# Tokens 0 to 127 of an expert gate built by indexed adds in DRAM instead of one-hot matmuls

## The chip, the cores and the metric

The kernel runs on one core of a Trainium2 chip. The metric is the device time of one launch in microseconds. Before the change it is 2061.44 us, the median of three runs (2060.55 to 2062.73).

## The reference

A decoder trunk of 256 tokens by 1024 features and 2 layers. Each layer has a mixer, a cross-attention and an expert block with 128 x 128 single-neuron experts, and 8 heads that choose 16 experts per token. The change is in the expert block:

```python
q = (xb @ w_pq).reshape(PEER_BLOCK, P_HEADS, 2, P_HALF)
sc = jnp.einsum('thpc,hpkc->thpk', q, sub_keys)
sv, si = lax.top_k(sc, TOPK)
cand = (sv[..., 0, :, None] + sv[..., 1, None, :]).reshape(..., TOPK * TOPK)
cid = (si[..., 0, :, None] * N_KEYS + si[..., 1, None, :]).reshape(..., TOPK * TOPK)
fv, fi = lax.top_k(cand, TOPK)
eid = jnp.take_along_axis(cid, fi, axis=-1)
g = jax.nn.softmax(fv, axis=-1)
a = gelu(einsum('thkd,td->thk', u_experts[eid], xb))
y = einsum('thk,thkd->td', g * a, v_experts[eid])
```

## The kernel before

The kernel does not gather experts. It computes the block densely: h = gelu(U x) for all 16384 experts, times a gate that is zero where a token did not choose an expert and the sum of its softmax weights where it did, times V. Weights come in slabs of 512 KB (128 partitions x 1024 float32), 340 a layer: 84 for the projections, 128 of U, 128 of V. SP loads them into a ring of four (`raw`). ACT rounds a slab to `w_hi` (fp32r), DVE makes the rest `w_lo` (`lo_part`, L848), and TensorE uses both: per U slab 8 chunks of one 512-column and one 256-column matmul (`wide_chunk`, L1345 and L1346), per V slab 12 matmuls of 512 columns (`expert_out`, L1733). The next slab into a ring place is asked for once its `lo_part` is through.

For each U slab ACT copies half of the sums to `h_out` (L721), DVE adds the other half (L1113), ACT applies gelu (L731), and SP stores 128 KB to `h_park` in DRAM. During V, SP loads these rows back into `h_in` (the first three into `early_in`), GpSimd multiplies each by its gate row (`gated`, L524), ACT and DVE split the product (L781, L1264), and TensorE uses it as the stationary operand.

The gate is `gate[column, row, token]` in SBUF, 128 KB per partition. While U streams, DVE finds the top 16 of the scores and of the candidate sums (`top16`), then decodes the row and the column of each choice with 16 comparisons (`pick`, L1198) and a tree of additions (L1206) for all 16 (token block, head) pairs at once, and makes the softmax weights (L1211 to L1213, semaphore `decoded`). Between these steps a helper `spend` puts the `lo_part`s into DVE's order: one whenever the estimated time of the other work has reached 1.56 us. At U slab `RET_AT` = 70 TensorE transposes rows, columns and weights (L1697, six 128x128). From slab `HOT_AT` = 72 on, DVE makes one-hot matrices for groups of 4 tokens (L1228, L1236, L1242), TensorE multiplies them (`gates_of`, L1708, 8 matmuls a group), and ACT copies the result to `gate` (L761). There are 64 groups a layer, in pairs, placed by `GROUP_AT` at fixed chunks of slabs 72 to 123: a pair every 13 chunks. The last four U slabs follow (L1339). TensorE, DVE, ACT, SP and GpSimd each have one order of instructions, written out in the program, and meet by semaphores.

GpSimd does little in U: after the sums of squares (L494), the load of `skT` (L507) and a scaling (L476) it waits for the last one-hot group, loads `par` (L516), and starts on `gated`.

Of the kernel before, what the change touches and what calls it, by code (L numbers as in the profile page):

```python
# [45 lines left out]
PH = 8  # L46
# [53 lines left out]
GROUPS = T // 4  # L100
HOT_AT = 72
RET_AT = 70
EXP_AT = 60
# [5 lines left out]
GROUP_AT = tuple(FIRST_PAIR + (n - n % 2) * HOT_SLABS * KB // GROUPS for n in range(GROUPS))  # L109
EARLY = RING - 1  # L110
H_SLOTS = 2
# [38 lines left out]
def trunk(nc, x, mem, slabs, params, sub_keys, out):  # L150
    ctx = ExitStack()
    with ctx:
# [32 lines left out]
        h_out = at("h_out", x_at + 6144, [P, H_SLOTS, T])  # L185
# [17 lines left out]
        pick_at = at("pick_at", top[0], [P, 2, T // 2, 2], FP16)  # L203
        g_parts = at("g_parts", top[0] + 2 * T * 2, [P, T // 2, PARTS, 2], FP16)
        top[0] += (2 + PARTS) * T * 2
        top[0] = (top[0] + LINE - 1) // LINE * LINE
        gated_at = top[0]
        gate = sb("gate", [P, NKEYS, T])
# [78 lines left out]

        h_park = nc.dram_tensor("h_park", (NKEYS, P, T), FP32, kind="Internal").ap()
# [7 lines left out]
        def sem(name):  # L296
            return ctx.enter_context(nc.semaphore(name))
# [39 lines left out]
        settled = sem("settled")  # L337
        act_step, dve_step, out_ready = sem("act_step"), sem("dve_step"), sem("out_ready")
# [12 lines left out]
        def _(sp):  # L351
# [26 lines left out]
            for layer in range(DEPTH):  # L378
# [10 lines left out]
                for j in range(RING):  # L389
                    next_slab(layer, U_AT, 0, j)  # L390
                    if j >= H_SLOTS:
                        store_h(layer, 0, j - H_SLOTS, j - H_SLOTS)
                with sp.Fori(1, U_SLABS // RING - 1) as g:
                    for j in range(RING):
                        next_slab(layer, U_AT, g, j)
                        store_h(layer, g, (j - H_SLOTS) % RING, j - H_SLOTS)
                last = U_SLABS // RING - 1
                for j in range(RING):
                    next_slab(layer, U_AT, last, j)
                    store_h(layer, last, (j - H_SLOTS) % RING, j - H_SLOTS)  # L400
# [9 lines left out]
                for j in range(H_SLOTS):  # L410
                    next_slab(layer, V_AT, 0, j)
                    store_h(layer, U_SLABS // RING, j, j - H_SLOTS)
# [7 lines left out]
                next_slab(layer, V_AT, 0, H_SLOTS)  # L420
# [37 lines left out]
        def _(pool):  # L458
# [11 lines left out]

            def scale(dst, count, evacs, xns):
# [25 lines left out]
            for layer in range(DEPTH):  # L497
# [7 lines left out]
                sum_chunks(layer, SUM_OUT, 0)  # L505
                pool.wait_ge(slab_done, layer * SLABS + XO_AT)
# [5 lines left out]
                settle(pool)  # L512

# [6 lines left out]
                def gated(g, j, h, n):  # L520
# [3 lines left out]
                    nc.gpsimd.tensor_tensor(h[:, n:n + 1, :], h[:, n:n + 1, :], gate[:, ds(g * RING + j, 1), :],  # L524
# [17 lines left out]
        def _(act):  # L542
# [73 lines left out]
            for layer in range(DEPTH):  # L616
# [89 lines left out]
                def gelu_out(at0, g, j):  # L706

                    act.wait_ge(slab_done, layer * SLABS + U_AT + at0 + g * RING + j + 1)
                    act.wait_ge(h_stored[j % H_SLOTS], (layer * (U_SLABS // H_SLOTS) + at0 // 2 + g * 2 + j // 2) * 16 + 16)
# [7 lines left out]
                def half_of(at0, g, j):  # L717

                    act.wait_ge(slab_done, layer * SLABS + U_AT + at0 + g * RING + j + 1)
                    act.wait_ge(h_stored[j % H_SLOTS], (layer * (U_SLABS // H_SLOTS) + at0 // 2 + g * 2 + j // 2) * 16 + 16)  # L720
# [30 lines left out]
                experts(RING, EXP_AT - RING)  # L751
                act.wait_ge(fin_ready, layer + 1)
                nc.scalar.activation(g_exp[:], g_exp[:], ACT.Exp).then_inc(gexp_ready, 1)
                experts(EXP_AT, HOT_AT - RING - EXP_AT)
# [4 lines left out]
                def gate_out(n):  # L759
                    act.wait_ge(gate_mm, layer * GROUPS + n + 2)  # L760
                    nc.scalar.activation(gate[:, :, 4 * n:4 * n + 4],  # L761
# [80 lines left out]
        def _(dve):  # L842
# [119 lines left out]
            for layer in range(DEPTH):  # L962
# [179 lines left out]
                for n in range(0, TB * SETS, 2):  # L1142
                    if n % SETS == 0:
                        dve.wait_ge(sc_evac, layer * TB + n // SETS + 1)
                        settle(dve)
                    src = (scores0, scores1)[n // SETS]
                    step.join()
                    top16(*[(src[:, m % SETS, :], struck[:, m - n, 0:NKEYS], top_v[:, m, :], top_u[:, m, :])
                            for m in (n, n + 1)], us=0.29)
                step.join()  # L1150
                step.mark(nc.vector.tensor_copy(top_i[:], top_u[:]))

                step.join()
                for b in range(TB):
                    tops = top_v[:, b * SETS:(b + 1) * SETS, :].rearrange("p (h s) a -> p h s a", s=2)
                    step.join()
                    first = 0
                    for a0, na, nb in CAND:
                        shape = [P, PH, na, nb]
                        step.mark(nc.vector.tensor_tensor(  # L1160
                            cand[:, :, first:first + na * nb].rearrange("p h (a b) -> p h a b", a=na),
# [3 lines left out]
                    spend(1.3)  # L1165
                    for n in range(b * PH, (b + 1) * PH, 2):
# [3 lines left out]
                step.join()  # L1170

                nc.vector.tensor_tensor(g_exp[:], fin_v[:], fin_v[:, :, 0:1].to_broadcast([P, TB * PH, TOPK]),
                                        ALU.subtract).then_inc(fin_ready, 1)
                flat_i = fin_i[:].rearrange("p c k -> p (c k)")
                step.mark(nc.vector.tensor_scalar(bit_u[:], flat_i, 8, None, ALU.bitwise_and))
                step.mark(nc.vector.tensor_scalar(low_u[:], flat_i, 7, None, ALU.bitwise_and))
                step.mark(nc.vector.tensor_scalar(by16_u[:], flat_i, 4, None, ALU.logical_shift_right))
# [638 lines left out]
```

## Time and profile before

| | us |
|---|---|
| median of three runs | 2061.44 |
| the profiled execution | 2061.37 |
| its span, first to last instruction | 2059.6 |
| TensorE busy | 2042.0 |
| DVE busy | 1643.4 |
| ACT busy | 1190.0 |
| GpSimd busy | 337.0 |

The profiled execution is within 0.1 us of the median, and 1.8 us of it lie outside the span. "Busy" counts an instruction from start to end, and matmuls overlap, so the durations of matmuls can't be added; the distance between starts says what one costs. All positions below are microseconds from the start of the span, in the first layer.

### The profile page before, as it was taken

What the parts mean: (1) busy time and instruction counts of PE and PEld (TensorE: products, weight loads), DVE (VectorE), ACT (ScalarE), POOL (GpSimd) and SP (SyncE); (2) the same over time, 40 slices, a digit from 0 to 9 for tenths busy, and PEclk for the clock granted to TensorE, in tenths of its full rate; (3) what the DMA queues carried; (4) which work ended last, traced back from release to release, by engine and by line L of the source; (5) the groups of instructions that cost most, each with busy time, mean ns of one, the idle gap of its engine ahead of it and who ended that gap; (6) DMA issues with size and microseconds to landing.
All of it is one profiled execution on the core that took longest, in us unless ns stands there. A gap on an engine that the chain in (4) does not pass through costs nothing.

```text
span 2059.6 us, 38391 instructions
## 1 busy us (share of the span) xinstructions
PE 2042.0 (99%) x11552; PEld 1756.4 (85%) x11552; DVE 1643.4 (80%) x3047; ACT 1190.0 (58%) x1901; POOL 337.0 (16%) x342
## 2 busy tenths in 40 slices
PE   8999999999999999999999999999999999999998
PEld 7888888888888888888888888888888898888886
DVE  7785869999998667767688858799999986776666
ACT  6655556667666555555565545666666665545553
POOL 3010110000000333335330102000000004333331
PEclk9999999999999999999999999999999999999999
DMA  6445456776555877777654555566665567777773
GB/s 232 148 154 175 172 193 237 236 233 216 196 199 196 265 241 241 262 241 242 211 188 135 186 170 169 195 237 236 223 215 197 200 215 255 240 241 262 242 241 124
DMA packets 174249, 435.54 MB, mean 211 GB/s; under 512 B 19504, under 2 KB 85040, under 8 KB 173136
## 3 DMA queue, kind: packets, MB, share of 16 engines
q1 hardware_dynamic: 173520, 430.06, 62.2%
q0 software_dynamic: 640, 4.32, 0.6%
q8 instruction: 53, 0.87, 0.2%
q14 instruction: 36, 0.29, 0.1%
HBM read 397.60 MB, written 36.70 MB: 211 GB/s over the span
## 4 chain that ended last, share of the span: by engine, by line
PE 93%; DVE 4%; ACT 1%; DMA 1%; issue 1%; SPq 0%; DVEq 0%; ACTq 0%
PE ps L1733 33%; PE ps L1345 32%; PE ps L1346 16%; PE ps L1708 3%; PE ps L1624 2%; PE ps L1339 2%; DVE w_lo L848 1%; DMA raw<-slabs 1%; PE ps L1755 1%; PE ps L1683 1%; PE ps L1649 1%; PE ps L1606 1%; ACT w_hi L725 0%; DMA h_park<-h_out 0%; DVE pick L1198 0%
## 5 line engine op out<-in xcount | busy, mean ns | idle before, releaser
L848 DVE TENSOR_TENSOR w_lo<-raw,w_hi 128x1024 fp32r<-128x1024 f32 x674 | 838.2, 1244 | 265.9 <-ACT w_hi L793 195.4
L1345 PE MATMUL ps<-act,w_hi 128*128 128x512 f32 x2784 | 986.0, 397 | 0.0
L1346 PE MATMUL ps<-act,w_lo 128*128 128x256 f32 x2784 | 776.4, 279 | 0.0
L1345 PEld LDWEIGHTS ps<-act,w_hi 128*128 128x128 f32 x2784 | 521.9, 187 | 115.2 <-issue 0.4
L1733 PE MATMUL ps<-w_hi,act 128*128 128x512 f32 x1936 | 596.4, 389 | 0.0
L1346 PEld LDWEIGHTS ps<-act,w_lo 128*128 128x128 f32 x2784 | 525.0, 189 | 0.3
L793 ACT ACTIVATE w_hi<-raw 128x1024 fp32r<-128x1024 f32 x248 | 263.1, 1061 | 326.8 <-PE ps L1733 326.8
L1733 PEld LDWEIGHTS ps<-w_hi,act 128*128 128x128 f32 x1936 | 363.4, 188 | 75.7
L1733 PE MATMUL ps<-w_lo,act 128*128 128x512 f32 x968 | 376.6, 389 | 0.0
L524 POOL TENSOR_TENSOR h_in<-h_in,gate 128x256 f32<-128x256 f32 x250 | 243.6, 976 | 437.5 <-DMA h_in<-h_park 437.5
L725 ACT ACTIVATE w_hi<-raw 128x1024 fp32r<-128x1024 f32 x248 | 261.1, 1053 | 0.0
L1733 PEld LDWEIGHTS ps<-w_lo,act 128*128 128x128 f32 x968 | 181.7, 188 | 37.5
L552 ACT ACTIVATE w_hi<-raw 128x1024 fp32r<-128x1024 f32 x168 | 177.1, 1054 | 47.9 <-PE ps L1346 26.6
L1264 DVE TENSOR_TENSOR act<-h_in,act 128x256 fp32r<-128x256 f32 x250 | 184.5, 738 | 4.9 <-ACT act L781 4.9
L731 ACT ACTIVATE h_out<-h_out 128x256 f32<-128x256 f32 x248 | 103.2, 416 | 124.6 <-DVE h_out L1113 122.8
L721 ACT ACTIVATE h_out<-ps 128x256 f32<-128x256 f32 x248 | 94.6, 382 | 120.5 <-PE ps L1346 106.8
L516 POOL DMA_DIRECT2D par<-params x2 | 1.2, 592 | 785.7 <-DVE hot_row L1242 785.7
L1113 DVE TENSOR_TENSOR h_out<-h_out,ps 128x256 f32<-128x256 f32 x248 | 102.1, 412 | 16.3 <-ACT h_out L721 16.0
L781 ACT ACTIVATE act<-h_in 128x256 fp32r<-128x256 f32 x250 | 100.0, 400 | 8.3 <-POOL h_in L524 8.3
L1242 DVE TENSOR_TENSOR hot_row<-row_is,g_parts 128x512 f16<-128x512 f16 x256 | 96.5, 418 | 0.0
L1345 PE MATMUL ps<-pre,w_hi 128*128 128x512 f32 x216 | 77.1, 400 | 0.0
L761 ACT ACTIVATE gate<-ps 128x512 f32<-128x512 f32 x128 | 70.4, 591 | 6.0 <-PE ps L1708 6.0
(268 smaller groups left out, 1818.3 us busy)
## 6 DMA issues: line engine op xcount, KB each, us to landing
raw<-slabs SPq DMA_DIRECT2D x680, 512.0 KB, 4.2
h_park<-h_out SPq DMA_DIRECT2D x256, 128.0 KB, 2.1
h_in<-h_park SPq DMA_DIRECT2D x250, 128.0 KB, 3.9
memT<-mem POOLq DMA_DIRECT2D x2, 1024.0 KB, 7.9
skT<-sub_keys POOLq DMA_DIRECT2D x2, 1024.0 KB, 6.3
x_park<-xT SPq DMA_DIRECT2D x2, 1024.0 KB, 6.4
xT<-x_park SPq DMA_DIRECT2D x2, 1024.0 KB, 7.3
xT<-x SPq DMA_DIRECT2D x4, 256.0 KB, 5.7
```

The lines of the kernel that those rows point to most:

```text
L524: nc.gpsimd.tensor_tensor(h[:, n:n + 1, :], h[:, n:n + 1, :], gate[:, ds(g * RING + j, 1), :], ALU.mult).then_inc(gated_ready, 1)
L552: nc.scalar.activation(w_hi[:, j].rearrange("p k c -> p (k c)"), raw[:, j, :], ACT.Copy).then_inc(hi_ready, 1)
L725: nc.scalar.activation(w_hi[:, j].rearrange("p k c -> p (k c)"), raw[:, j, :], ACT.Copy).then_inc(hi_ready, 1)
L731: nc.scalar.activation(slot, slot, ACT.Gelu).then_inc(act_evac, 1)
L781: nc.scalar.activation(hi[:, j:j + 1, :], h[:, j:j + 1, :], ACT.Copy).then_inc(ga_hi_ready, 1)
L793: nc.scalar.activation(w_hi[:, j].rearrange("p k c -> p (k c)"), raw[:, j, :], ACT.Copy).then_inc(hi_ready, 1)
L848: nc.vector.tensor_tensor(w_lo[:, j].rearrange("p k c -> p (k c)"), raw[:, j, :], w_hi[:, j].rearrange("p k c -> p (k c)").bitcast(FP32), ...
L1113: nc.vector.tensor_tensor(slot, slot, ps[:, n % RING:n % RING + 1, 0:T], ALU.add).then_inc(u_sum, 1)
L1264: nc.vector.tensor_tensor(lo[:, j:j + 1, :], h[:, j:j + 1, :], hi[:, j:j + 1, :].bitcast(FP32), ALU.subtract).then_inc(ga_ready, 1)
L1345: nc.tensor.matmul(ps[:, j, :], w_hi[:, j, k, :], a[:, :, k, :], start=(k == 0), stop=False)
L1346: return nc.tensor.matmul(ps[:, j, hi * T:hi * T + T], w_lo[:, j, k, :], a[:, hi, k, :], start=False, stop=(k == KB - 1))
L1733: last = nc.tensor.matmul(ps[:, 2 * b + half, :], a[:, j, b * P:(b + 1) * P], w[:, j, 4 * half:4 * half + 4, :].rearrange("p k c -> p (k c)"),
```

## The change

Tokens 0 to 127 no longer pass through one-hot matmuls. A DRAM buffer `g_spread` of 128 x 128 x 128 floats holds their gate. GpSimd fills it with zeros (8 DMAs of 1 MB, each waited for) while the attention's slabs run. DVE works the choices off in three parts (`CHOICES`): heads 0 and 1 of the first token block, heads 2 to 7 of it, then all 8 heads of the second block. For the first block it also computes a flat address for each choice, (column x 128 + row) x 128 + token, and the plain softmax weight. GpSimd then issues 16 indirect DMAs a head, each adding 128 weights of 4 bytes (one a token) into `g_spread`, 128 DMAs a layer, and waits for all 16 after each head. The buffer comes back in 8 pieces of 1 MB (16 gate rows each): piece 0 and 1 before the gating starts, the others one piece ahead of the rows that use them. `gate` is now laid out as two token halves. The second half still goes through one-hot matmuls: 32 groups in place of 64, in slabs 80 to 123, a pair every 22 chunks; three transposes in place of six, at slab 78. `h_out` has four slots in place of two and lies in the part of `gate` that piece 6 fills later; SP still stores with a lag of two slabs.

```diff
-GROUPS = T // 4
-HOT_AT = 72
-RET_AT = 70
-EXP_AT = 60
+GROUPS = P // 4
+HOT_AT = 80
+RET_AT = 78
+CHOICES = ((0, 0, 2), (0, 2, PH), (1, 0, PH))
+EXP_ATS = (12, 36, 72)
...
-H_SLOTS = 2
+H_SLOTS = 4
+H_LAG = 2
...
-        gate = sb("gate", [P, NKEYS, T])
+        gate = sb("gate", [P, TB, NKEYS, P])
...
+                nc.gpsimd.memset(zeros[:], 0.0).then_inc(zeros_set, 1)
+                pool.wait_ge(zeros_set, layer + 1)
+                for i in range(NKEYS // ZERO_ROWS):
+                    pool.dma_start(spread[:, i * ZERO_ROWS:(i + 1) * ZERO_ROWS, :], zeros[:]).then_inc(zeroed, 16)
+                    pool.wait_ge(zeroed, layer * (NKEYS // ZERO_ROWS * 16) + (i + 1) * 16)
...
+                for h in range(PH):
+                    for p in range(2):
+                        if h == CHOICES[p][1]:
+                            pool.wait_ge(place_ready, layer * 4 + 2 * p + 2)
+                    for i in range(h * TOPK, (h + 1) * TOPK):
+                        nc.gpsimd.indirect_dma_start(g_spread, bass.IndirectOffsetOnAxis(ap=place_u[:, i:i + 1], axis=0),
+                                                     g_flat[:, i:i + 1], None, compute_op=ALU.add).then_inc(scattered, 16)
+                    pool.wait_ge(scattered, (layer * PH + h + 1) * (TOPK * 16))
...
+                load_back(0)
+                loaded_back(0)
+                load_back(1)
...
-                with pool.Fori(1, V_SLABS // RING) as g:
-                    for j in range(RING):
-                        gated(g, j, h_in, j)
+                for i in range(BACKS):
+                    if i < BACKS - 1:
+                        loaded_back(i + 1)
...
+                    if i < BACKS - 2:
+                        load_back(i + 2)
+                    with pool.Fori(max(1, i * BACK_ROWS // RING), (i + 1) * BACK_ROWS // RING) as g:
+                        for j in range(RING):
+                            gated(g, j, h_in, j)
...
+                    if b == 0:
+                        dve.wait_ge(consts, 5)
+                        nc.vector.tensor_scalar(place_u[:, own], place_f[:, own], float(P), tok[:, 0:1],
+                                                ALU.mult, ALU.add).then_inc(place_ready, 1)
+                        nc.vector.tensor_tensor(g_flat[:, own].rearrange("p (c k) -> p c k", k=TOPK), g_exp[:, cs], of_sum,
+                                                ALU.mult).then_inc(place_ready, 1)
```

GpSimd's order from the attention's sums to the first gated rows of layer 1. Before:

```order
22 L494 TENSOR_TENSOR sq_sum<-sq 128x256 [waits sq_chunk]
23 L494 TENSOR_TENSOR sq_sum<-sq_sum,sq 128x256 [waits summed,sq_chunk] x5
24 L507 DMA skT<-sub_keys 128x2048 [waits slab_done]
25 L494 TENSOR_TENSOR sq_sum<-sq 128x256 [waits sq_chunk]
26 L494 TENSOR_TENSOR sq_sum<-sq_sum,sq 128x256 [waits summed,sq_chunk] x5
27 L476 TENSOR_TENSOR qpT<-qpT,rstd_pre 128x256 [waits act_evac,xn_ready]
28 L476 TENSOR_TENSOR qpT<-qpT,rstd_pre 128x256 x7
29 L516 DMA par<-params 128x124 [waits act_ready,hot_row_ready]
30 L524 TENSOR_TENSOR early_in<-early_in,gate 128x256 [waits gate_copied,h_loaded0]
```

Now (the last two rows are the scatter's first head, and seven more follow):

```order
25 L526 MEMSET zeros 128x2048
26 L529 DMA g_spread<-zeros 128x2048 [waits zeros_set]
27 L529 DMA g_spread<-zeros 128x2048 [waits zeroed] x7
28 L532 DMA skT<-sub_keys 128x2048 [waits slab_done,zeroed]
29 L513 TENSOR_TENSOR sq_sum<-sq 128x256 [waits sq_chunk]
30 L513 TENSOR_TENSOR sq_sum<-sq_sum,sq 128x256 [waits summed,sq_chunk] x5
31 L495 TENSOR_TENSOR qpT<-qpT,rstd_pre 128x256 [waits act_evac,xn_ready]
32 L495 TENSOR_TENSOR qpT<-qpT,rstd_pre 128x256 x7
33 L544 DMA g_spread<-g_flat,place_u 2097152x1 [waits act_ready,place_ready]
34 L544 DMA g_spread<-g_flat,place_u 2097152x1 x15
```

and behind the last head:

```order
49 L550 DMA gate<-g_spread 128x2048 [waits scattered]
50 L550 DMA gate<-g_spread 128x2048 [waits spread_back]
51 L562 DMA par<-params 128x124 [waits hot_row_ready]
52 L571 TENSOR_TENSOR early_in<-early_in,gate 128x256 [waits gate_copied,h_loaded0]
53 L571 TENSOR_TENSOR early_in<-early_in,gate 128x256 [waits h_loaded1]
```

Between the scaling and the load of `par` there now stand 128 indirect DMAs and two 1 MB loads; the stores of zeros stand ahead of `skT` and the sums.

DVE's order at the end of the choices, where the weights for TensorE's transposes are made (`w_lo` is `lo_part`; the one in row 668 is that of slab 70). Before:

```order
667 L1113 TENSOR_TENSOR h_out<-h_out,ps 128x256 [waits u_half]
668 L848 TENSOR_TENSOR w_lo<-raw,w_hi 128x1024 [waits hi_ready]
669 L1211 TENSOR_REDUCE g_sum<-g_exp 128x16 [waits gexp_ready,dve_step]
670 L1212 RECIPROCAL g_sum<-g_sum 128x16 [waits dve_step]
671 L1213 SCALAR_TENSOR_TENSOR g_exp<-g_exp,g_sum 128x256 [waits dve_step]
672 L1113 TENSOR_TENSOR h_out<-h_out,ps 128x256 [waits u_half]
673 L848 TENSOR_TENSOR w_lo<-raw,w_hi 128x1024 [waits hi_ready]
674 L1113 TENSOR_TENSOR h_out<-h_out,ps 128x256 [waits u_half]
675 L848 TENSOR_TENSOR w_lo<-raw,w_hi 128x1024 [waits hi_ready]
676 L1219 CAST pick_at<-ps 128x512 [waits ret_mm]
677 L1221 CAST g_parts<-ps 128x128x2
```

Now (the `lo_part` in row 744 is that of slab 77):

```order
743 L1174 TENSOR_TENSOR h_out<-h_out,ps 128x256 [waits u_half]
744 L909 TENSOR_TENSOR w_lo<-raw,w_hi 128x1024 [waits hi_ready]
745 L1300 TENSOR_TENSOR col_f<-pick 128x128 [waits dve_step]
746 L1213 TENSOR_REDUCE g_sum<-g_exp 128x8 [waits gexp_ready,dve_step]
747 L1214 RECIPROCAL g_sum<-g_sum 128x8 [waits dve_step]
748 L1223 SCALAR_TENSOR_TENSOR g_exp<-g_exp,g_sum 128x128 [waits dve_step]
749 L1174 TENSOR_TENSOR h_out<-h_out,ps 128x256 [waits u_half]
750 L909 TENSOR_TENSOR w_lo<-raw,w_hi 128x1024 [waits hi_ready]
751 L1174 TENSOR_TENSOR h_out<-h_out,ps 128x256 [waits u_half]
752 L909 TENSOR_TENSOR w_lo<-raw,w_hi 128x1024 [waits hi_ready]
753 L1174 TENSOR_TENSOR h_out<-h_out,ps 128x256 [waits u_half]
754 L909 TENSOR_TENSOR w_lo<-raw,w_hi 128x1024 [waits hi_ready]
755 L1308 CAST pick_at<-ps 128x256 [waits ret_mm]
```

The reduction `g_sum` to `decoded` (L1213, now L1223) stands behind the `lo_part` of slab 70 before and of slab 77 now; two `lo_part`s more stood between it and `pick_at`, and now there are three.

DVE's order at the place where the first two heads are handed to GpSimd, behind 13 `lo_part`s of the U stretch; before, nothing of the choices was decoded there:

```order
350 L1174 TENSOR_TENSOR h_out<-h_out,ps 128x256 [waits u_half]
351 L909 TENSOR_TENSOR w_lo<-raw,w_hi 128x1024 [waits hi_ready]
352 L1210 SCALAR_TENSOR_TENSOR place_f<-col_f,row_f 128x32 [waits dve_step]
353 L1213 TENSOR_REDUCE g_sum<-g_exp 128x2 [waits gexp_ready]
354 L1214 RECIPROCAL g_sum<-g_sum 128x2 [waits dve_step]
355 L1218 TENSOR_SCALAR place_u<-place_f,tok 128x32 [waits consts,dve_step]
356 L1220 TENSOR_TENSOR g_flat<-g_exp,g_sum 128x32
357 L1174 TENSOR_TENSOR h_out<-h_out,ps 128x256 [waits u_half]
358 L909 TENSOR_TENSOR w_lo<-raw,w_hi 128x1024 [waits hi_ready]
359 L1187 MAX top_v<-scores_120 128x8 [waits dve_step]
```

Four small instructions and the addresses stand between two `lo_part`s. The same five rows come again for heads 2 to 7, 27 `lo_part`s later.

## Rows read from the trace of the kernel before

**Rows 1.** The page, part 1: busy time, share of the span, number of instructions.

```profile
PE 2042.0 (99%) x11552; PEld 1756.4 (85%) x11552; DVE 1643.4 (80%) x3047; ACT 1190.0 (58%) x1901; POOL 337.0 (16%) x342
```

**Rows 2.** Busy time by stretch: from:to, length, engines, clock, DMA share, GB/s.

```profile
core 0: us, PE busy (x) PEld busy (x) DVE busy (x) ACT busy (x) POOL busy (x), PEclk, DMA share, GB/s
146.00:208.00 62.00, 62.00 (x324) 53.04 (x323) 41.09 (x53) 32.08 (x53) 0.17 (x1) 1.00 0.49 161
301.00:484.00 183.00, 183.00 (x1058) 161.35 (x1058) 170.87 (x540) 118.67 (x199) 0.00 (x0) 1.00 0.68 228
492.00:664.70 172.70, 172.64 (x1325) 151.88 (x1324) 163.87 (x356) 118.37 (x219) 0.59 (x1) 1.00 0.58 199
700.00:1000.00 300.00, 300.00 (x1325) 248.43 (x1324) 213.81 (x221) 151.01 (x221) 113.99 (x111) 1.00 0.73 245
840.00:860.00 20.00, 20.00 (x89) 16.54 (x89) 13.39 (x15) 9.83 (x15) 5.67 (x7) 1.00 0.85 287
```

**Rows 3.** The chain that ended last: start, length, what; four one-hot pairs.

```profile
537.27 0.93 PE ps L1708 x16
542.77 0.93 PE ps L1708 x16
...
658.27 0.93 PE ps L1708 x16
...
663.77 0.93 PE ps L1708 x16
```

**Rows 4.** The same chain: the six transposes at slab 70.

```profile
484.16 0.66 PE ps L1697 x6
```

**Rows 5.** Timeline of TensorE: the first V matmul.

```profile
678.19 0.40 PE L1733 MATMUL ps<-w_hi,early_hi 128*128 128x512 f32 x1
```

**Rows 6.** Timeline of GpSimd: start, length, operation, [idle before, releaser].

```profile
140.77 1.47 POOL L494 TENSOR_TENSOR sq_sum<-sq_sum,sq 128x256 f32<-128x256 f32 x1 [1.30 <-ACT sq L588]
207.82 0.59 POOL L507 DMA_DIRECT2D skT<-sub_keys  x1 [65.58 <-PE ps L1624]
223.07 0.80 POOL L494 TENSOR_TENSOR sq_sum<-sq 128x256 f32<-128x256 f32 x1 [14.65 <-ACT sq L588]
...
663.11 0.59 POOL L516 DMA_DIRECT2D par<-params  x1 [392.93 <-DVE hot_row L1242]
669.54 3.42 POOL L524 TENSOR_TENSOR early_in<-early_in,gate 128x256 f32<-128x256 f32 x3 [5.84 <-DMA early_in<-h_park]
681.66 0.74 POOL L524 TENSOR_TENSOR h_in<-h_in,gate 128x256 f32<-128x256 f32 x1 [8.70 <-DMA h_in<-h_park]
```

**Rows 7.** DMA issues: queue, count, KB each, median us to landing.

```profile
raw<-slabs SPq DMA_DIRECT2D x680, 512.0 KB, 4.2
...
skT<-sub_keys POOLq DMA_DIRECT2D x2, 1024.0 KB, 6.3
x_park<-xT SPq DMA_DIRECT2D x2, 1024.0 KB, 6.4
...
par<-params POOLq DMA_DIRECT2D x2, 62.0 KB, 3.1
```

**Rows 8.** Timeline of DVE, slabs 62 to 72: comparisons, tree, weights, first copy.

```profile
443.00 1.09 DVE L1198 SCALAR_TENSOR_TENSOR pick<-a_at,top_i 128x256 bf16<-128x256 bf16 x3
...
476.29 1.23 DVE L1206 TENSOR_TENSOR pick<-pick 128x2048 bf16<-128x2048 bf16 x1
...
482.62 0.42 DVE L1213 SCALAR_TENSOR_TENSOR g_exp<-g_exp,g_sum 128x256 f32<-128x256 f32 x1
482.96 0.41 DVE L1113 TENSOR_TENSOR h_out<-h_out,ps 128x256 f32<-128x256 f32 x1
483.30 1.22 DVE L848 TENSOR_TENSOR w_lo<-raw,w_hi 128x1024 fp32r<-128x1024 f32 x1
...
487.00 0.68 DVE L1219 CAST pick_at<-ps 128x512 f16<-128x512 f32 x1
```

**Rows 9.** The weight remainder on DVE, in 700 to 1000, then 310 to 480.

```profile
L848 DVE TENSOR_TENSOR w_lo<-raw,w_hi 128x1024 fp32r<-128x1024 f32 x110 | 138.8, 1262 | 86.1 <-ACT w_hi L793 86.0
...
L848 DVE TENSOR_TENSOR w_lo<-raw,w_hi 128x1024 fp32r<-128x1024 f32 x60 | 73.3, 1222 | 5.2 <-ACT w_hi L725 4.7
```

More of the change, by code:

```diff
@@ L399, in _ @@
                     next_slab(layer, U_AT, last, j)
-                    store_h(layer, last, (j - H_SLOTS) % RING, j - H_SLOTS)
+                    store_h(layer, last, (j - H_LAG) % RING, j - H_LAG)
                     if j == 0:
@@ L750, in _ @@
                 scores_out(1, scores1)
[L751 to L754, printed above, removed]
+                at = RING
+                for p, (b, h0, h1) in enumerate(CHOICES):
+                    exp_at = EXP_ATS[p]
+                    experts(at, exp_at - at)
+                    act.wait_ge(fin_ready, layer * len(CHOICES) + p + 1)
+                    chosen = g_exp[:, b * PH + h0:b * PH + h1, :]
+                    nc.scalar.activation(chosen, chosen, ACT.Exp).then_inc(gexp_ready, 1)
+                    at = exp_at
+                experts(at, HOT_AT - RING - at)
                 for j in range(RING - 1):
@@ new lines, in _ @@
+                for p, (b, h0, h1) in enumerate(CHOICES):
+                    src = (scores0, scores1)[b]
+                    if h0 == 0:
+                        dve.wait_ge(sc_evac, layer * TB + b + 1)
+                        settle(dve)
+                    heads = h1 - h0
+                    wide = heads / PH
+                    for n in range(b * SETS + 2 * h0, b * SETS + 2 * h1, 2):
+                        step.join()
+                        top16(*[(src[:, m % SETS, :], struck[:, m - n, 0:NKEYS], top_v[:, m, :], top_u[:, m, :])
+                                for m in (n, n + 1)], us=0.29)
+                        if p > 0 and n == b * SETS + 2 * h0:
+                            step.join()
+                            weights(p - 1)
+                            spend(0.9)
+                    step.join()
+                    sets = slice(b * SETS + 2 * h0, b * SETS + 2 * h1)
+                    step.mark(nc.vector.tensor_copy(top_i[:, sets, :], top_u[:, sets, :]))
+                    tops = top_v[:, sets, :].rearrange("p (h s) a -> p h s a", s=2)
@@ new lines, in _ @@
+                    spend(0.6 + 0.8 * wide)
+                    keys = top_i[:, sets, :].rearrange("p (c s) a -> p c s a", s=2)
+                    for side, (place, found) in enumerate(((a_at, row_f), (b_at, col_f))):
+                        step.join()
+                        for a in range(TOPK):
+                            step.mark(nc.vector.scalar_tensor_tensor(
+                                pick[:, a, cs], place[:, flat].rearrange("p (c k) -> p c k", k=TOPK), float(a),
+                                keys[:, :, side, a].unsqueeze(2).to_broadcast([P, heads, TOPK]), ALU.is_equal, ALU.mult))
+                            spend(0.08 + 0.16 * wide)
+                        n = TOPK // 2
+                        while n:
+                            step.join()
+                            out = (found[:, flat].rearrange("p (o c k) -> p o c k", o=1, k=TOPK) if n == 1
+                                   else pick[:, 0:n, cs])
+                            step.mark(nc.vector.tensor_tensor(out, pick[:, 0:n, cs], pick[:, n:2 * n, cs], ALU.add))
+                            spend(0.07 * n * wide + 0.2)
+                            n //= 2
@@ L1216, in _ @@
+                    step.join()
+                weights(len(CHOICES) - 1)
                 while due[0] < HOT_AT + 1:
```

158 lines of the change are left out of this document (83 added, 75 removed).

## The prediction

> **What bounds the kernel now.** I read the engines' totals first: TensorE is busy for 2042.0 of 2059.6 us [rows 1]. Then the stretches: in each of the four long ones TensorE is busy throughout or all but 0.06 us, at full granted clock, in both halves of the U stream, at its middle and in V [rows 2]. So what counts is what TensorE has to do, and whether anything new makes it wait. DVE is close behind in the U stream: 170.9 of 183.0 us up to the transposes, 163.9 of 172.7 us in the one-hot stretch [rows 2]. GpSimd is idle for 393 us ahead of the load of `par` [rows 6], and the DMA engines are 0.49 to 0.73 busy [rows 2]. All figures are of layer 1; layer 2 repeats it, so each is doubled at the end.
>
> **What the change takes off TensorE.** Two one-hot pairs start 5.50 us apart (537.27 and 542.77) [rows 3], with 13 chunks between them. A chunk follows from rows 2: 183.0 us hold 1058 matmuls, which is 529 chunks, 0.346 us each, so 13 take 4.50 us and a pair costs 1.00 us. (The matmuls alone show 0.93; the rest is the slower restart behind them.) A layer loses 16 of 32 pairs: 16.0 us. Three of six transposes go: half of 0.66 us [rows 4], 0.33. Sum 16.33 us a layer, 32.7 us for both. Nothing else on TensorE changes. This is on the path that sets the end, since that engine has no other idle time to give it back to.
>
> **What it adds, part by part.** First I place the new steps in time. A slab is 8 chunks, 2.77 us. The transposes stand at slab 70, 484.16 [rows 4], so slab 4 starts at 484.2 - 66 x 2.77 = 301.4, slab 17 at 337.4 and slab 44 at 412.2. DVE hands over heads 0 and 1 behind the `lo_part` of slab 16, and heads 2 to 7 behind that of slab 43, so about then or a few us earlier. V starts at 678.2 now [rows 5], and at 661.9 after. GpSimd gates its first rows at 669.5 [rows 6], 8.7 us ahead of V; that becomes 653.2. Piece 0 must have landed by then, and a 1 MB load takes 6.3 us [rows 7], so the scatter has to end by about 646.
>
> *The scatter.* No row shows an indirect or adding DMA. Let c be what one costs GpSimd's order; each head ends with a wait for its last one, for which I take the 3.1 us in which the small `par` load lands [rows 7]. All heads: 646 - 337.4 = 308.6, less 8 x 3.1 = 24.8, over 128: c may be 2.2 us. The last six heads alone: 646 - 412.2 = 233.8, less 18.6, over 96: 2.2 us as well. The bounds of c: the issue of `skT`, with as many partition rows (128), takes 0.59 us [rows 6], and that is the low end. The high end is 3.1 us, if no transfer overlapped the next. I take 0.59 for the descriptors and 0.74 for a pass that reads operands on GpSimd (the shortest gating multiply [rows 6]): 1.33 us, nearer to the low rows, because the issue is the same kind of work and only a head's end is waited for. Then heads 2 to 7 take 96 x 1.33 + 18.6 = 146 us and end at 558, 88 us before they must. Cost on the path: 0, hidden by U slabs 17 to 123. With c over 2.2 the cover is gone, and every 0.1 us costs 12.8 us a layer.
>
> The Trainium skill speaks against this part. Its page "DMA: Bandwidth & Descriptors" (section Bandwidth) gives about 10.5 ns a packet for small transfers from GpSimd; at 144 packets (128 and 16 completions, my estimate from that page) one indirect DMA would take 1.5 us, still below 2.2. Its page "SBUF — State Buffer" (Who interferes with whom) says that descriptor generation is starved while DVE is in a two-port mode, and that GpSimd's reads contend with DVE instructions with two SBUF inputs. No row here has such a DMA beside DVE.
>
> *DMA engines.* From rows 2, a busy share times 16 engines times the length is engine time. In 146 to 208: 0.49 x 16 x 62 = 486 us for 22.4 slabs of 128 rows, 0.170 us per 4 KB row. In 301 to 484: 0.68 x 16 x 183 / 66 = 30.2 us a slab; less 128 x 0.170, 8.4 us are left for the 128 rows of 1 KB of `h_park`, 0.066 us each. A 4-byte row is thus between 0.03 (the line through both) and 0.07 us, doubled if the read-back for the add counts like a second one: 0.03 to 0.14. With completions an engine gets 1152 of them a layer: 35 to 161 us; I take 0.07, 81 us, the measured row that it is nearest to. Free are (1 - 0.68) x 146.8 + (1 - 0.58) x 161.8 = 115 us until 646. It fits; at over 0.10 us a packet it would not.
>
> *Zeros.* 8 stores of 1 MB, each waited for. The like store `x_park` lands in 6.4 us [rows 7]; with issue and wait some 8, so 64 us from 142 (behind the sum at 140.77) to 206 to 210. The load of `skT` at 207.8 may come a little later, and is used in the scores at about 283; the next sums start at 223 [rows 6]. The stores have 81 us, so up to 10 us each. Their engine time is about 2.5 us per 8 us (0.31 us per 8 KB row, the same line), which lifts the share from 0.49 to about 0.8: 0 us on the path.
>
> *Pieces back.* Six during V, one per 16 slabs: +0.06 on a share of 0.73. The precedent is the 1 MB load of `xT` in V: share 0.85 in 840 to 860, TensorE busy for all 20.00 us [rows 2]. 0 us, with a doubt at the start of V, where piece 2 meets the first `h_in` rows.
>
> *DVE.* The `pick` comparison takes 0.335 us in a row of three (1.09 - 0.42, over 2) [rows 8]; with 1.04 ns per element (1222 against about 420 ns for 1024 and 256 elements, rows 8 and 9) the fixed part is 0.07. For widths 32, 96 and 128 it is 0.10 + 0.17 + 0.20 = 0.47 in place of 0.335, 32 times: +4.3 us. The trees, with their waits, come three times at smaller widths: about +4; decode, weights and addresses about +4. Sum +12 us a layer (0 to 18). Against it the stretch to the transposes is 8 slabs longer, and each gives 2.77 - 1.47 (one remainder and one half sum, 1.14 + 0.33) = 1.3 us: +10.4, on top of 12.1 us idle now. So DVE has about 10 us left. `decoded` follows the `lo_part` of slab 77 by about 1.6 us, less than slab 77 takes, so it is not waited for long. In the one-hot stretch DVE falls from 95% to about 80%. A GpSimd operation beside DVE stretches a remainder from 1222 to 1262 ns [rows 9]; 128 times 0.04 is 5 us, and still fits.
>
> *Four slots, gate layout.* ACT's short waits for stores fall away; TensorE never waited for them, and the ACT copy has the same size. 0.
>
> *What I charge.* For the sum of small waits at the scatter's bursts, the hand-over at slab 78 and the start of V, half a slab a layer, 1.4 us, 3 for both (0 to 12).
>
> **Sum.** On the profiled execution's own time, 2061.4: 2061.4 - 32.7 + 3 = 2031.7 us. The median of the runs is the same to 0.1 us, so I predict 2032.
>
> **Rivals.**
> A. The scatter comes late and the change loses. Place: the first wait of `gated` on piece 0; TensorE stands before V slab 0. It decides from c = 2.2 + 16.3 / 128 = 2.33 us on (slower), and between 2.2 and 2.33 the gain shrinks. At the high end, c = 3.1, heads end at 337 + 397 + 25 = 759, 113 us late: 2061.4 - 32.7 + 226 = 2255. At 2.6 it is 2061 - 33 + 102 = 2131. For it: the waits per head, the two-input work of a nearly full DVE beside it, and no row for the operation. Against: 0.59 us for as many rows, and 0.9 us of reserve in my c.
> B. The DMA engines fill up. At 0.14 us a packet they would need 161 us where 115 are free. Slab loads, landing in 4.2 us [rows 7], then come late during the scatter. If the 46 us are shared half with the slabs, in which TensorE stands for a third, some 8 us a layer: 2045. For it: tiny adds; against: two queues, and the slab ring is four deep.
> C. DVE is late in the U stretch (extra work 18 us, and longer by GpSimd's use of the ports): 18 + 5 - 22.5 is about 1, and if every issue held DVE for its whole 0.59 us, 75 us against 10 of reserve, so that nothing is gained: 2061 or more. Between the two I take 10 us a layer: 2049. For it: 93% busy now. Against: the 40 ns of rows 9.
>
> **How the numbers follow.** Forecast 0.62, its own range 2027 to 2040 (no charge, up to 12 charged). A 0.15, nearly all slower. B 0.12 and C 0.11, mostly faster by less, with 0.04 of them within 0.2% and 0.03 slower. A measurement here tells 0.2%, 4 us. Faster 0.62 + 0.16 = 0.78; same 0.05 (0.01 from A); slower 0.17. Range: from 2026, just below no charge, up through B and C to 2058; left out is what lies in A and the worst of C.
>
> **What would show it.** Right: L1795 with 512 matmuls and pairs 8.6 us apart; TensorE busy for all but about 20 us of the span; indirect DMAs 1 to 2 us apart, their last head done before 646; the early rows gated near 653; the first V matmul near 662 to 664. A would show as TensorE idle before the first V matmul with GpSimd still at L544. B would show as ACT waiting for `raw` while the scatter runs, C as TensorE waiting for `w_lo` or `decoded` in slabs 5 to 80. I would be wrong in the other direction only if a removed pair were worth more than 1.00 us.

## The result and the profile after

The changed kernel takes 2048.05 us (median of four runs, 2047.54 to 2049.61). On the same chip the kernel before takes 2062.09 us (four runs, 2060.55 to 2063.97). The ratio is 0.9933 with a 95% interval of 0.9916 to 0.995. So it is faster, by 14.0 us, and not by the 30 forecast. The profiled execution took 2049.61 us, its span 2047.9.

The totals of the page, to be held against [rows 1]: columns are busy time, share of the span and number of instructions.

```profile
PE 2021.5 (99%) x11034; PEld 1731.2 (85%) x11034; DVE 1585.5 (77%) x3025; ACT 1230.3 (60%) x1901; POOL 823.8 (40%) x633
```

ACT has 1901 instructions as before, though 64 of its 128 gate copies are gone, and it is busy 40 us longer. The chain that ended last now leaves TensorE, which had 93% of it before:

```profile
PE 75%; DVE 14%; ACT 5%; issue 3%; DMA 2%; SPq 0%; ACTq 0%; DVEq 0%; POOL 0%; POOLq 0%
```

Where this happens is in the stretches that answer to [rows 2]: same columns; the stretch in which the zeros are stored, U up to the transposes, 20 us of it, most of the one-hot stretch, and 20 us of V.

```profile
core 0: us, PE busy (x) PEld busy (x) DVE busy (x) ACT busy (x) POOL busy (x), PEclk, DMA share, GB/s
146.00:208.00 62.00, 61.95 (x323) 52.96 (x323) 40.88 (x52) 31.82 (x53) 3.73 (x7) 1.00 0.80 295
301.00:516.00 215.00, 210.70 (x1180) 181.54 (x1180) 194.52 (x671) 167.87 (x256) 136.12 (x74) 0.99 0.82 218
400.00:420.00 20.00, 18.52 (x103) 15.43 (x102) 18.05 (x61) 15.84 (x25) 6.91 (x5) 1.00 0.68 196
510.00:660.00 150.00, 150.00 (x1017) 130.90 (x1016) 122.18 (x234) 96.97 (x180) 104.12 (x60) 0.99 0.84 226
840.00:860.00 20.00, 20.00 (x90) 16.57 (x89) 13.86 (x15) 10.41 (x16) 8.20 (x8) 1.00 0.91 317
```

TensorE is idle for 4.3 of 215 us in the U stretch, where it was idle for none of 183 before. ACT's share there is 0.78 (167.87 of 215), against 0.65 in [rows 2]. The waits of TensorE between 290 and 690 us name ACT (total us, times, longest us):

```profile
PE ps L1434 <- ACT h_out L787: 4.0, 6, 1.8
PE ps L1434 <- DVE w_lo L909: 0.3, 1, 0.3
```

What ACT does more of is in its groups by line (count, busy time, mean ns, idle before). First of before, then of the changed kernel, where L777 is the copy (L721 before), L787 the Gelu (L731) and L813 the Exp (L753):

```profile
L721 ACT ACT_TABLE_LOAD x6 | 7.7, 1283 | 0.1
L731 ACT ACT_TABLE_LOAD x6 | 7.7, 1283 | 0.1
...
L753 ACT ACT_TABLE_LOAD x2 | 2.6, 1283 | 0.0
```

```profile
L777 ACT ACT_TABLE_LOAD x34 | 43.6, 1283 | 0.6
L787 ACT ACT_TABLE_LOAD x34 | 43.6, 1283 | 0.6
...
L813 ACT ACT_TABLE_LOAD x6 | 7.7, 1283 | 0.1
```

The Exp needs a table of its own, and the change issues it three times a layer in place of once. The four new Exps explain four loads at L813 and four at L787, for Gelu's table to come back, eight in all. But there are 60 more than before, 77 us of them. (With the four Exps they make up for the 64 gate copies that are gone, so that the count stays at 1901.) ACT's timeline, from one Exp to the start of the next round of four slabs, shows the rest (start, length, what, idle before):

```profile
397.62 1.28 ACT L813 ACT_TABLE_LOAD   x1
398.92 0.28 ACT L813 ACTIVATE g_exp<-g_exp 128x96 f32<-128x96 f32 x1
399.22 1.28 ACT L777 ACT_TABLE_LOAD   x1
400.51 0.39 ACT L777 ACTIVATE h_out<-ps 128x256 f32<-128x256 f32 x1
400.79 1.05 ACT L781 ACTIVATE w_hi<-raw 128x1024 fp32r<-128x1024 f32 x1
401.86 1.28 ACT L787 ACT_TABLE_LOAD   x1
403.16 0.42 ACT L787 ACTIVATE h_out<-h_out 128x256 f32<-128x256 f32 x1
...
411.01 1.28 ACT L777 ACT_TABLE_LOAD   x1
```

There is one load ahead of the first copy behind the Exp and another ahead of the first Gelu; the copies behind them have none. At 411.01, when the loop's next round begins, a table is loaded ahead of the copy again with no Exp in between, and Gelu's again at 413.65. The load ahead of the copy is not one that the copy needs: where the same slabs are written out (experiment 1), the copy behind the Exp runs without it. It comes with the loop. That a body, being one piece of code, starts with a load which every round then repeats is how I read this; the program that was built was not looked at. In before, two rounds a layer of this loop stood behind the Exp at slab 60. In the changed kernel there are 16: six from slab 12, nine from slab 36, one from slab 72. Each line has one load a layer besides, at the start of U, which makes 3 and 17, and 6 and 34 for both layers.

### The profile page after: what moved, and what is told of

The parts are those of the page before. It is cut to its first block, busy times and chain, and to the rows that moved or that the text cites. A ratio compares the mean times of both kernels' runs of the same rounds, so it can differ in the third digit from the quotient of the medians.

```text
span 2047.9 us, 37662 instructions
## 1 busy us (share of the span) xinstructions
PE 2021.5 (99%) x11034; PEld 1731.2 (85%) x11034; DVE 1585.5 (77%) x3025; ACT 1230.3 (60%) x1901; POOL 823.8 (40%) x633
## 4 chain that ended last, share of the span: by engine, by line
PE 75%; DVE 14%; ACT 5%; issue 3%; DMA 2%; SPq 0%; ACTq 0%; DVEq 0%; POOL 0%; POOLq 0%
PE ps L1820 33%; PE ps L1434 22%; PE ps L1435 11%; DVE w_lo L909 5%; PE ps L1713 2%; ACT w_hi L781 2%; PE ps L1795 1%; DVE h_out L1174 1%; DMA raw<-slabs 1%; PE ps L1428 1%; DVE pick L1291 1%; ACT h_out L777 1%; PE ps L1842 1%; PE ps L1772 1%; PE ps L1695 1%
## 5 line engine op out<-in xcount | busy, mean ns | idle before, releaser
L544 POOL DMA_INDIRECT g_spread<-g_flat,place_u x256 | 470.9, 1840 | 279.6 <-DVE g_flat L1220 149.2
L787 ACT ACTIVATE h_out<-h_out 128x256 f32<-128x256 f32 x248 | 103.0, 415 | 106.1 <-DVE h_out L1174 104.6
L777 ACT ACTIVATE h_out<-ps 128x256 f32<-128x256 f32 x248 | 93.4, 376 | 78.8 <-PE ps L1435 78.4
L513 POOL TENSOR_TENSOR sq_sum<-sq 128x256 f32<-128x256 f32 x4 | 4.5, 1138 | 184.4 <-ACT sq L644 184.4
L1435 PE MATMUL ps<-pre,w_lo 128*128 128x256 f32 x216 | 60.4, 280 | 0.0
```

The lines of the kernel that those rows point to most:

```text
L544: nc.gpsimd.indirect_dma_start(g_spread, bass.IndirectOffsetOnAxis(ap=place_u[:, i:i + 1], axis=0), g_flat[:, i:i + 1], None, compute_op=A ...
L777: nc.scalar.activation(h_out[:, j % H_SLOTS:j % H_SLOTS + 1, :], ps[:, j:j + 1, T:2 * T], ACT.Copy).then_inc(u_half, 1)
L1435: return nc.tensor.matmul(ps[:, j, hi * T:hi * T + T], w_lo[:, j, k, :], a[:, hi, k, :], start=False, stop=(k == KB - 1))
```

## The experiments

Nine kernels ran, in three groups, each beside runs of the kernel before on its chip (2062.64, 2061.78 and 2060.90 us). "Rounds" are passes of ACT's loop over four slabs.

**1. The rounds behind the first two Exps start in another way.** The four slabs behind each are written out ahead of the loop, so the loop begins with Gelu's table in place:

```
 nc.scalar.activation(chosen, chosen, ACT.Exp).then_inc(gexp_ready, 1)
 at = exp_at
+if p < len(CHOICES) - 1:
+    for j in range(RING):
+        half_of(at, 0, j)
+        gelu_of(at, 0, j)
+    at += RING
```

> The changed kernel, with one edit: the four slabs behind each of the first two Exps stand outside the loop on ACT, so that the loops begin with the gelu table in place. Theory 1 (ACT reloads its activation table twice in every loop round behind an Exp, 68 loads of 1.28 us in place of 12 in the U streams, and this holds up the chain of ACT, DVE and TensorE): the loads fall to 20, TensorE reaches the transposes near 508 in place of 516.6 in layer 1, and the time falls to about 2034 us (2029 to 2040), the rest being the scatter, which then ends too late for piece 0 by 1 to 3 us a layer. Theory 2 (the adds hold up the slab loads): 2044 or more. Theory 3 (DVE's narrower decode is the excess): 2044 or more.

Measured: 2032.47 us (four runs, 2028.12 to 2035.31), ratio 0.9851 (0.9828 to 0.9873). The loads are down, and the chain is TensorE's again:

```profile
L787 ACT ACT_TABLE_LOAD x8 | 10.3, 1283 | 0.1
...
L777 ACT ACT_TABLE_LOAD x4 | 5.1, 1283 | 0.1
```

```profile
PE 98%; DVE 2%; ACT 0%; DMA 0%; issue 0%; SPq 0%; DVEq 0%; ACTq 0%
```

The same work, adds, waits and Exps, gives the forecast time once the reloads are out: they are worth 15.6 us. This is also the version that beats both kernels. The forecast of 20 loads was too high, there are 12 at these two lines: behind the Exps that are followed by written-out slabs only Gelu loads a table (start, length, what).

```profile
394.62 0.28 ACT L813 ACTIVATE g_exp<-g_exp 128x96 f32<-128x96 f32 x1
394.81 0.36 ACT L777 ACTIVATE h_out<-ps 128x256 f32<-128x256 f32 x1
...
396.14 1.28 ACT L787 ACT_TABLE_LOAD   x1
```

Nor does the scatter end too late here: TensorE has no wait at the start of V in either layer.

**2. No adds.** The 128 indirect adds a layer and their waits go, the reloads stay. This kernel leaves out the gates of tokens 0 to 127, which stay zero.

```
-for i in range(h * TOPK, (h + 1) * TOPK):
-    nc.gpsimd.indirect_dma_start(g_spread, ..., g_flat[:, i:i + 1], None, compute_op=ALU.add)
-pool.wait_ge(scattered, ...)
```

> The changed kernel without the 256 indirect adds and the waits for them (the gate of tokens 0 to 127 stays zero); the table reloads stay. Theory 1 (table reloads): the transposes stay near 515, only the 1.7 us wait at the start of V and ACT's waits for slabs go, so 2040 to 2046 us. Theory 2 (adds crowd the DMA engines or GpSimd's issues hold DVE): 2030 to 2034. Theory 3 (narrow decode): 2040 or more.

Measured: 2052.83 us (2050.94 to 2054.95), ratio 0.9951 (0.9933 to 0.9969). Nothing is gained, so theory 2 falls: no cost of the adds on TensorE shows. The forecast of 2040 to 2046 was missed as well, since this kernel is 4.0 us slower than the changed one on the same chip (experiment 7), and their ranges don't meet. Of this, TensorE's waits for ACT and DVE behind the start of U account for 2.3 us (11.6 us in this profile, 9.3 in that of 7); why they are longer without the adds is open.

**3. Both edits.** It leaves out the same gates.

> Both edits: no table reloads in the loops, and no adds (the gate of tokens 0 to 127 stays zero). What is left over above 2029 us (2061.4 less the 32.7 of removed matmuls) is the price of the narrower decode on DVE, of the zeros and of the pieces. Theory 1: 2029 to 2032. Theory 3 (narrow decode on DVE): 2040 or more. The difference to the kernel with the first edit alone is what the adds cost once nothing else is in the way: theory 1 says 2 to 6 us, theory 2 over 10.

Measured: 2034.51 us (2029.8 to 2036.28), ratio 0.9853 (0.9833 to 0.9873). That is 2.0 us above experiment 1, with ranges that overlap, where theory 1 had it 2 to 6 us below: so no cost of the adds is left once the reloads are out, and no second cost of the change shows behind the first.

**4. The reloads alone, in the kernel before.** Two Exps of one column are put at slabs 12 and 36 and nothing else is changed:

```
-experts(RING, EXP_AT - RING)
+experts(RING, 12 - RING)
+nc.scalar.activation(warm[:], eps[:], ACT.Exp)
+experts(12, 36 - 12)
+nc.scalar.activation(warm[:], eps[:], ACT.Exp)
+experts(36, EXP_AT - 36)
```

> The kernel before, with two Exps of one element added on ACT at slabs 12 and 36, which split its loop there as in the changed kernel; nothing else changes. Theory 1: 12 loop rounds now reload two tables each, some 33 us more on ACT a layer, and the time rises by 8 to 25 us, to 2070 to 2087. Theories 2 and 3: two instructions and two tables, 5 us of ACT a layer with idle time to take it: 2062.

Measured: 2079.78 us (2078.63 to 2080.05), ratio 1.0078 (1.0062 to 1.0095), so 17.1 us slower than before on that chip.

```profile
L721 ACT ACT_TABLE_LOAD x30 | 38.5, 1283 | 0.7
L731 ACT ACT_TABLE_LOAD x30 | 38.5, 1283 | 0.5
```

The cost appears with none of the change's other parts there. 24 rounds over both layers reload that did not in before, so a round costs 0.71 us here.

**5. Writing slabs out where there is little to save.** A control: the kernel before with the four slabs behind its own Exp written out.

> The kernel before, with the four slabs behind its one Exp written out ahead of the loop. It has 6 loads each of the copy's and the Gelu's table at 1.28 us in its loop lines; 4 of each should stay. Table theory: what counts is not a load but a load in every round of a long loop; here three rounds become one, about 2 rounds a layer at some 0.55 us, so 2060 to 2062. Rival (writing the slabs out helps by itself, by fewer branches or another pace, whatever the tables): before would gain as much as the changed kernel did, about 15 us, 2047.

Measured: 2062.52 us (ten runs, 2060.3 to 2065.95), ratio 0.9998 (0.9989 to 1.0008). Writing slabs out is not worth the 15 us of the rival by itself. It did take loads away, more than I had forecast: two are left at L721 and four at L731, in place of six and six, since the written-out copy needs none. What these six loads cost is too little to be seen within the interval (from 2.3 us faster to 1.6 us slower).

**6. A middle dose.** Experiment 1, but the slabs are written out behind the second Exp alone (`if p == 1:` in place of the condition above).

> The changed kernel with the slabs behind the second Exp alone written out; six rounds a layer behind the first Exp keep their two loads. Table theory: the cost goes by the number of such rounds. 16 rounds a layer cost 15.6 us over both layers, 0.5 us each, so 6 a layer keep 6: 2038. Rival (one stall at one place, such as the one at the transposes with the clock fall behind it): the rounds behind the second Exp are ahead of the transposes, so nearly all of the 15.6 us go with them, 2033, or none, 2048.

Measured: 2037.92 us (2037.51 to 2039.1), ratio 0.9882 (0.9865 to 0.9898), where the table theory had 2038, and neither 2033 nor 2048, which the rival had. The doses over both layers, by their loads at L777: 4, 16 and 34 of them, and 2032.5, 2037.9 and 2048.4 us (the mean of two medians). The steps are 5.4 us for 12 rounds and 10.5 us for 18: 0.45 to 0.58 us a round, of 2.57 us of loads in it. The rest of the loads is hidden: without them ACT has 0.35 of its time free. That the number came out to 0.1 us is in part luck. In this run's profile TensorE waits for ACT or DVE in the U streams for only 0.9 us in all, and in layer 1 it runs at the slower of the two paces that are told of at the end, 115 matmuls in 340 to 360 us with no wait in the U stream. How much of the 5.4 us is the 12 rounds' and how much the pace's is open; the step of 10.5 us doesn't hang on it.

**7. The changed kernel again,** on the chip of 5, 6 and 8.

> The changed kernel itself, on the chip of the other three, so that their distances from it are read without a change of chip: 2048, and 34 loads of each table.

Measured: 2048.8 us (2046.02 to 2050.07), ratio 0.993 (0.9913 to 0.9947), with 34 loads at each line. On this chip the distance to experiment 1 is 16.3 us, in place of 15.6 from the first four runs.

**8. Two slots for the sums.** Experiment 1 with `H_SLOTS = 2`.

> The changed kernel with both groups of slabs written out, and two slots for sums of the first matrix in place of four (the lag of the store stays two). My step had four slots worth nothing: then 2032 to 2034. Rival: with the adds beside the stores, the stores land later and ACT waits for them, which the four slots cover; then TensorE waits with it, 2040 or more. In the trace the wait to read is ACT's for the store of the same slot.

Measured: 2039.39 us (2037.96 to 2041.2), ratio 0.9888 (0.9871 to 0.9904): 6.9 us above experiment 1, and the ranges don't meet. ACT's waits between 290 and 660 us show the store:

```profile
ACT h_out L777 <- DMA h_park<-h_out: 30.6, 34, 3.7
```

In the same window of experiment 1 ACT has no such wait. So the four slots may not be worth the zero that I gave them: without them the kernel of experiment 1 is 7 us slower. How this gets to TensorE is open. Its own waits in 290 to 690 us come to 0.3 us, and its pace in this profile is the slower one told of at the end (115 matmuls in 340 to 360 us), which could be all of the 6.9.

**9. Rival A, made to happen.** Experiment 1 with all eight heads handed over at once, so the adds start late (GpSimd's wait for the hand-over is changed to fit):

```
-CHOICES = ((0, 0, 2), (0, 2, PH), (1, 0, PH))
-EXP_ATS = (12, 36, 72)
+CHOICES = ((0, 0, PH), (1, 0, PH))
+EXP_ATS = (36, 68)
```

> The changed kernel with the slabs behind the Exp written out, and all eight heads handed over at once, so the adds of the first two heads can't start ahead of about slab 44, 412 us (the second Exp moves from slab 72 to 68, since DVE comes to it sooner). This makes rival A happen on purpose. With 2.14 us an add and 3.8 us a head's end, eight heads take 8 x (34.2 + 3.8) = 304 us and end at 716 in place of 643; the load of piece 0 follows, and V starts near 735 in place of 663.5. If each us behind the deadline costs a us: 72 a layer, 2032 + 144 = 2176. If the late start is cushioned (the adds go faster once DVE and the slab loads stand still): 2100 to 2150. If the adds did not set the start of V at all: 2032.

Measured: 2117.3 us (two runs, 2114.64 and 2119.96), ratio 1.0274 (1.0243 to 1.0306). GpSimd's timeline: the first add, the last, and the load of the first piece; under it TensorE's longest wait in 600 to 780 us.

```profile
395.43 2.71 POOL L543 DMA_INDIRECT g_spread<-g_flat,place_u  x1 [125.46 <-DVE g_flat L1224]
...
691.61 1.56 POOL L543 DMA_INDIRECT g_spread<-g_flat,place_u  x1 [0.30 <-issue]
694.90 0.61 POOL L549 DMA_DIRECT2D gate<-g_spread  x1 [1.73 <-DMA g_spread<-g_flat,place_u]
```

```profile
PE ps L1824 <- issue: 42.6, 1, 42.6
```

The mechanism is there: V starts at 704.0 in place of 663.5, and the time is 84.8 us above experiment 1, of which TensorE's waits at the start of V make 81.3 (42.6 and 38.7). (The profile puts the wait down to "issue"; GpSimd's rows show what was missing.) The forecast was 59 us too high, for two reasons in the main. DVE hands over at 395 and not at 412, since it decodes one set and not two. And piece 0 needs to be asked for only 9.1 us ahead of V (694.90 to 704.0), while in experiment 1 it is 16.3 us ahead (647.19 to 663.5): 7.2 us, which I had left out. Piece 0 is asked for 47.7 us later than in experiment 1; less 7.2 that is 40.5, which is what V's start shows in layer 1. Not all of the 7.2 us was idle reserve: GpSimd waits 4.9 us for piece 0 here, where the slab loads stand still, and 8.3 us in experiment 1, where they don't.

## Why the prediction was wrong

**The step that failed is the one on ACT.** "What it adds, part by part" lists adds, zeros, pieces, DVE, slots. The three Exps have no entry. ACT's own entry is its waits for stores and its copy to `gate`, priced at 0. The Exps, and any table that they load, were put at nothing without a reason; ACT's busy share, 118.67 of 183 us in [rows 2], looked like room enough. In their place the runs showed 60 more table loads, most of them in 16 rounds a layer of ACT's loop. What that is worth is 15.6 us (experiment 1 against the changed kernel), and with it the forecast of 2032 comes out at 2048. No rival covered it: C gave nearly the measured time, 2049, but by work of DVE's own, and experiment 1 has all of that work without the loss. The trace of before had the sign: six loads at each of L721 and L731 for two Exps. The start of U and one Exp can explain at most two loads a layer at each line; three is the sign of the loop.

**How a half-idle engine came to count.** ACT's rows of 215 us have 47 us free, and its loads come 2.57 us at a time. In a round each slab has 2.77 us, of which ACT needs about 1.8, so by my estimate a slab with both loads is late by 1.6 us. DVE waits for ACT's copy before its own half of the sum, and has only 20.5 us free of 215. The chain between 404 and 409 us is DVE's alone (start, length, what):

```profile
404.71 0.33 DVE h_out L1174
405.04 1.14 DVE w_lo L909
406.18 0.28 DVE pick L1300
...
407.70 0.32 DVE h_out L1174
408.02 1.14 DVE w_lo L909
```

So DVE's lateness is made up slowly, and the next round's loads are there before it is. Some of the loss comes after a stall: TensorE stands 1.83 us before 509.48, and from 511.0 to 514.2 its granted clock is 0.50, the lower level of 1.2 GHz (the PEclk column of the last row below). There its pairs take 0.64 us each, as between the second and third row, in place of 0.35. Five pairs make 1.4 us.

```profile
509.48 0.47 PE L1434 MATMUL ps<-act,w_hi 128*128 128x512 f32 x1 [1.83 <-ACT h_out L787]
...
512.29 0.63 PE L1434 MATMUL ps<-act,w_hi 128*128 128x512 f32 x1
...
512.93 0.63 PE L1434 MATMUL ps<-act,w_hi 128*128 128x512 f32 x1
...
514.58 0.40 PE L1434 MATMUL ps<-act,w_hi 128*128 128x512 f32 x1
```

```profile
511.00:514.20 3.20, 3.20 (x12) 2.72 (x11) 3.10 (x7) 1.76 (x4) 2.90 (x2) 0.50 1.00 209
```

The 4.3 us of waits and these 1.4 us are 5.7 of the 9.8 us by which the transposes are late in layer 1, against experiment 1. The other 4 us are of the size of the slower pace, at which this run goes and the profile of experiment 1 does not. That this is the chain's path was read, not tried; that the loads set the loss off was tried (1, 4, 6).

**The other steps.**

*TensorE's saving, 32.7 us, charge 3.* Right. Experiment 1 is 30.2 us below before. In its chain the one-hot pairs stand 8.8 and 8.6 us apart by turns (the first two below), against 5.50 in [rows 3]:

```profile
524.17 0.94 PE ps L1800 x16
532.93 0.94 PE ps L1800 x16
```

Its transposes are at 506.9 and V starts at 663.5, where my count of slabs has 506.3 and 661.9. In the changed kernel they are at 516.7 and 673.2, so the loss lies ahead of the transposes: from there to V both kernels take 156.5 us. One more wait of the changed kernel's profile lies elsewhere: in layer 2 TensorE stands 1.7 us early in V, where GpSimd waits 10.3 us for the first row of `h_in` from DRAM. It is in the place of my doubt about the start of V, but experiments 1 and 7 don't have it.

*The scatter.* That it costs nothing on the path was right, the size was not. The issues of the changed kernel, whole program and then its end in layer 1, which answer to [rows 6]:

```profile
L544 POOL DMA_INDIRECT g_spread<-g_flat,place_u x256 | 470.9, 1840 | 279.6 <-DVE g_flat L1220 149.2 <-issue 92.9 <-DMA g_spread<-g_flat,place_u 37.5
```

```profile
641.49 1.56 POOL L544 DMA_INDIRECT g_spread<-g_flat,place_u  x1 [0.30 <-issue]
646.73 0.60 POOL L550 DMA_DIRECT2D gate<-g_spread  x1 [3.68 <-DMA g_spread<-g_flat,place_u]
...
665.62 3.29 POOL L571 TENSOR_TENSOR early_in<-early_in,gate 128x256 f32<-128x256 f32 x3 [9.83 <-DMA early_in<-h_park]
```

One add holds GpSimd for 1.84 us and 0.30 between: c is 2.14 us, not 1.33 (2.2 over heads 2 to 7, with some longer gaps). The wait at a head's end is 1.7 to 3.9 us in layer 1, 3.0 in the mean, where I had 3.1. Of the 88 us of reserve at most 7 were there (experiment 9). I had leaned toward the row of a plain issue (0.59 us), and the operation took three times that. The bound, c up to 2.2 us, was in the right place: the adds took nearly that, and the first piece was asked for at 646.73, where my deadline was 646 and my forecast for the end of the adds 558. That the zero held with so little left is luck, as far as the size of c goes. The estimate from "DMA: Bandwidth & Descriptors" (Bandwidth) in the Trainium skill was 1.5 us, low too. (The 144 packets of that estimate are right: the changed kernel has 36864 packets on GpSimd's queue that the kernel of experiment 3 lacks, for 256 adds.)

*DMA engines.* Rival B fell: the share in 301 to 506 is 0.85 in experiment 1 with TensorE busy for 205.00 of 205.00 us, and without the adds (2, 3) no time is gained. The packets cost about half of what I took: from 337 to 646 us the share is 0.85 in experiment 1 and 0.71 in experiment 3, so 0.14 of 309 us, 43 us an engine or 0.04 us a packet, where I had 81 and 0.07.

*Zeros and pieces.* Right at 0. TensorE is busy for 61.95 of 62 us beside the zeros, at a DMA share of 0.80 as forecast, and for all of 840 to 860. In the stretches of V shown and in experiment 1 no piece makes it wait.

*DVE.* Right. In experiment 1 (the row below has the columns of the windows above) it is busy for 193.70 of 205 us up to the transposes, so 11.3 are left, where I had 10. Rival C fell by itself; but by my reading a nearly full DVE is why ACT's lateness reached TensorE.

```profile
301.00:506.00 205.00, 205.00 (x1187) 179.38 (x1187) 193.70 (x675) 134.10 (x228) 134.60 (x71) 1.00 0.85 230
```

*Rival A.* It did not come, by at most 7 us a layer. It was closer than my 88 us made it.

## What to carry to other kernels

Before an activation is added to or moved in an engine's loop, count the loads of its function tables in the profile, line by line, and hold them against the number of times that the function changes. Here there were more loads than changes, because a loop behind the odd function reloaded in each round, and writing out the first round behind that function took the loads away (68 to 12). And a free share of an engine is an average: ACT was 0.35 free, but its loads came 2.57 us at a time, ahead of a DVE that was itself 0.90 busy, and the time rose by 15.6 us.

## What the runs showed of the hardware

A table load takes 1.283 us each time, and the activation behind it starts within 0.02 us (399.22 + 1.28, then 400.51). The Trainium skill, "ScalarE: Activation LUTs" (What ACT_TABLE_LOAD costs), has the same 1283 ns for the load, and a drain of 1380 ns beside it, 2.66 us in all. No drain shows in these rows, ahead of a load or behind it; by an estimate from the 2.66 us, two loads in a round would have been 5.3 us, where the rows have 2.57. The Trainium skill, "ScalarE activation tables: per-element evaluation and per-set limits" (Table sets in the compiler and the runtime), says that the loads are placed per block of code. The timeline above agrees: Gelu and then a copy stand at 403.16 and 403.48 with no load between, and the same two at 410.57 and 412.30, across the rounds, with one.

An indirect add of 128 values of 4 bytes holds GpSimd for 1.55 us at the least, in the rows read here. In the full U stream it takes longer. Both are in the kernel of experiment 9, first in 420 to 520 us with DVE busy for 88.66 of 100 and a DMA share of 0.85, then in 660 to 694 with DVE busy for none of it, TensorE for 1.43 us, and a DMA share of 0.19. Whether DVE or the slab loads make the difference was not tried. The rows, in that order:

```profile
L543 POOL DMA_INDIRECT g_spread<-g_flat,place_u x40 | 78.6, 1964 | 21.9 <-issue 11.3 <-DMA g_spread<-g_flat,place_u 10.6
```

```profile
L543 POOL DMA_INDIRECT g_spread<-g_flat,place_u x16 | 24.9, 1555 | 9.3 <-issue 7.5 <-DMA g_spread<-g_flat,place_u 1.8
```

TensorE has two paces in the U stream at full granted clock, with no wait in either: 117 or 118 matmuls in 20 us, or 115. The pairs themselves stand 0.347 and 0.353 us apart. The first row is experiment 1, the second experiment 3, at 340 to 360 us of each:

```profile
340.00:360.00 20.00, 20.00 (x118) 17.48 (x117) 19.75 (x71) 12.22 (x22) 16.65 (x12) 1.00 0.95 234
```

```profile
340.00:360.00 20.00, 20.00 (x115) 17.35 (x114) 19.56 (x67) 12.33 (x23) 0.00 (x0) 1.00 0.79 251
```

In experiment 7 the pace is 117 at 340 us, and 115 at 440 us behind the stall. 2% of about 200 us is 4 us a layer, which is the size of the spread between runs of one kernel (2028 to 2035 in experiment 1). So the difference between two single profiles, 18.6 us of span between the changed kernel and experiment 1, is larger than that of the medians, 15.6, and only the medians are compared here. What sets the pace was not tried.
